# One fused transformer kernel on one core: the row scale of the mixer's norm applied after the products, the state stage's sums and exponentials made earlier

## The reference

```python
hn = rmsnorm(h, norm_mix_w[i])
proj = hn @ w_in[i]
q, k, v, z, xbc, dt_raw = jnp.split(proj, SPLITS, axis=-1)
att = chunk_band_attention(q, k, v, rel_bias[i])
ssd = ssd_mixer(z, xbc, dt_raw, conv_w[i], conv_b[i], dt_bias[i], a_log[i], d_skip[i], ssd_norm_w[i])
h = h + jnp.concatenate([att, ssd], axis=-1) @ w_out[i]
hn = rmsnorm(h, norm_mlp_w[i])
h = h + jnp.square(jax.nn.relu(hn @ w_ff1[i])) @ w_ff2[i]
```

## Time and profile before

| | us |
|---|---|
| median of 3 runs | 781.71 |
| the runs | 780.65, 781.71, 781.85 |
| the profiled execution | 780.67 |
| its span | 778.9 |
| TensorE busy in the span | 762.0 |
| DVE busy | 513.8 |
| ACT busy | 416.0 |
| POOL busy | 98.3 |

### The profile page before, as it was taken

One profiled execution on the slowest core, in us unless ns is written; L12 is line 12 of the kernel. 1 busy time (PEld: TensorE's weight loads), 2 busy tenths in 40 slices (PEclk: granted clock), 3 DMA queues, 4 the chain that ended last, 5 costly groups with the idle time before them and its releaser, 6 DMA issues.

```text
span 778.9 us, 12960 instructions
## 1 busy us (share of the span) xinstructions
PE 762.0 (98%) x5014; PEld 670.3 (86%) x5014; DVE 513.8 (66%) x816; ACT 416.0 (53%) x623; POOL 98.3 (13%) x74
## 2 busy tenths in 40 slices
PE   8999999999999999999999899999999999999997
PEld 7998877799978887999787699889777999999996
DVE  6985556666664558477866875787856755555554
ACT  5544445453664553446675567576655544444443
POOL 3341000000100004111300207700000000000002
PEclk9999999999999999999999999999999999999999
DMA  9965643344664544676833554765317575656541
GB/s 334 332 203 177 215 163 108 122 157 121 210 224 160 172 157 160 195 227 197 247 114 104 166 176 151 219 205 173 109 55 219 192 237 191 207 177 211 169 156 55
DMA packets 77659, 139.54 MB, mean 179 GB/s; under 512 B 7184, under 2 KB 15648, under 8 KB 77600
## 3 DMA queue, kind: packets, MB, share of 16 engines
q1 hardware_dynamic: 75744, 132.15, 52.4%
q0 software_dynamic: 1856, 6.57, 2.6%
HBM read 134.90 MB, written 1.06 MB: 175 GB/s over the span
## 4 chain that ended last, share of the span: by engine, by line
PE 87%; DVE 6%; issue 3%; POOL 2%; ACT 1%; DMA 1%; SPq 0%; POOLq 0%; ACTq 0%; DVEq 0%
PE acc L1081 13%; PE acc L1083 13%; PE acc L1082 13%; PE acc L1089 12%; PE acc L1091 12%; PE acc L1090 12%; DVE w_lo L810 2%; PE acc L1369 1%; PE acc L1403 1%; DMA raw<-in_w_in_even 1%; PE acc L1342 1%; PE acc L1282 1%; PE acc L1238 1%; PE acc L1353 1%; POOL b_lo L810 1%
## 5 line engine op out<-in xcount | busy, mean ns | idle before, releaser
L810 DVE TENSOR_TENSOR w_lo<-raw,w_hi 128x1024 fp32r<-128x1024 f32 (+1 forms) x224 | 275.3, 1245 | 171.3 <-ACT w_hi L790 90.2
L1089 PE MATMUL acc<-x_hi,w_hi 128*128 128x256 f32 x840 | 234.8, 280 | 1.5 <-DVE w_lo L810 1.1
L1091 PE MATMUL acc<-x_hi,w_lo 128*128 128x256 f32 x840 | 232.1, 276 | 0.0
L1090 PE MATMUL acc<-x_lo,w_hi 128*128 128x256 f32 x840 | 232.1, 276 | 0.0
L790 ACT ACTIVATE w_hi<-raw 128x1024 fp32r<-128x1024 f32 (+1 forms) x128 | 133.6, 1045 | 126.4 <-PE acc L1091 63.9
L780 ACT ACTIVATE w_hi<-raw 128x1024 fp32r<-128x1024 f32 x109 | 116.1, 1065 | 107.6 <-PE acc L1091 55.5
L1089 PEld LDWEIGHTS acc<-x_hi,w_hi 128*128 128x128 f32 x840 | 157.7, 188 | 4.1 <-issue 2.8
L1090 PEld LDWEIGHTS acc<-x_lo,w_hi 128*128 128x128 f32 x840 | 157.8, 188 | 0.8 <-issue 0.5
L1091 PEld LDWEIGHTS acc<-x_hi,w_lo 128*128 128x128 f32 x840 | 157.7, 188 | 0.0
L1081 PE MATMUL acc<-w_hi,cat_hi 128*128 128x512 f32 x272 | 108.9, 400 | 0.2 <-DVE w_lo L810 0.2
L1083 PE MATMUL acc<-w_hi,cat_lo 128*128 128x512 f32 x272 | 106.2, 390 | 0.0
(11 more groups left out here) (297 smaller groups left out, 903.0 us busy)
## 6 DMA issues: line engine op xcount, KB each, us to landing
raw<-in_w_ff SPq DMA_DIRECT2D x32, 1024.0 KB, 5.3
raw<-in_w_in_even SPq DMA_DIRECT2D x28, 1024.0 KB, 5.0
raw<-in_w_in_odd SPq DMA_DIRECT2D x16, 1024.0 KB, 5.4
raw<-in_w_in SPq DMA_DIRECT2D x16, 1024.0 KB, 5.6
raw<-in_w_out_even SPq DMA_DIRECT2D x12, 1024.0 KB, 5.4
raw<-in_w_out SPq DMA_DIRECT2D x4, 1024.0 KB, 5.3
raw<-in_w_in_even SPq DMA_DIRECT2D x4, 512.0 KB, 6.2
raw<-in_w_ukv_even SPq DMA_DIRECT2D x8, 256.0 KB, 3.2
```

The costliest lines, as they stand in the source:

```text
L810: ins = eng.tensor_tensor(lo, r, hi.bitcast(F32), ALU.subtract)
L1089: pe.matmul(o, wh[k][:, fs], hi[:, ka, :], start=start and f % 2 == 0, stop=False, skip_group_check=True)
L1090: pe.matmul(o, wh[k][:, fs], lo[:, ka, :], start=False, stop=False, skip_group_check=True)
L1091: ins = pe.matmul(o, wl[k][:, fs], hi[:, ka, :], start=False, stop=stop, skip_group_check=True)
```

## The change

The order of the plan and the place of two kinds of work change.

1. r is no longer applied to the rows ahead of the transposes. TensorE turns `res` itself; the products of v, dt, xBC, z, q and k are made from unscaled rows, and r enters where a chunk is read out of PSUM: as a per-row scale for v, z, dt and y·silu(z); as `r_row` (r spread over all partitions by one product with a diagonal, `mix_spread`) for q, k and xBC. Those read-outs of xBC, q and k go from ACT to DVE.
2. `v_rows` takes v's products with the high parts apart from those with the low parts; dt is made once, with 256 columns. The five filling products at the start go, the one ahead of the second transposes become four.
3. `ssd_cums` moves to c1, the four spreads (`ssd_spread`) behind it, into four buffers that lie over `cat2`. The decays of group 0 (`ssd_seg` 0) are made behind the last `conv_end`, those of group 1 behind z0b and ahead of z0's `epi`, 2 and 3 one and two pieces on. C·B, x and every near group lie a piece sooner; the far part lies inside z1b.
4. The norm of y is in two steps (`ssd_gate`, `ssd_scale`), its transposes lie in kb instead of V; some of the splits of weights wait until these steps are issued.

The diff, cut:

```diff
 RAW_SLOTS = 3
 WARM = 9
-BUSY_MIX = (5, 1)
+BUSY_MIX = 4
 LAG = 3
...
     step("mix_turn", 1)
-    step("rows_of", (rows_pieces["dt"], 0, 0, 8))
     step("rows_of", (rows_pieces["v"], 1, 0, 8))
     step("epi", rows_pieces["v"].chunk)
     step("rows_of", (rows_pieces["dt"], 1, 0, 8))
...
         if n:
             step("conv", 2 * (n - 1))
+            if n == 1:
+                step("ssd_cums", 0)
         else:
+            step("mix_spread", 0)
             step("dt_sum", c_dt)
             step("epi", c_dt)
             step("softplus", 0)
             step("conv", 2 * (n - 1) + 1)
         if n == 1:
             step("conv_end", 0)
+            step("ssd_spread", 0)
         if n == 2:
             step("conv", 4)
             step("conv_end", 1)
     parts[0]()
     step("conv", 5)
     step("conv_end", 2)
+    step("ssd_seg", 0)
     parts[1]()
     z_end = steps.pop()
-    step("ssd_cums", 0)
+    step("ssd_xs", 0)
+    step("ssd_seg", 1)
     steps.append(z_end)
-    between = [[("ssd_cb", 0), ("ssd_xs", 0), ("ssd_xs", 1)], [("ssd_rows", 0)], [("ssd_rows", 1)], [("ssd_rows", 2)], [("ssd_rows", 3)],
-               [("ssd_last", 0), ("ssd_gate", 0)], [("ssd_turn", 0)]]
+    between = [[("ssd_cb", 0), ("ssd_rows", 0), ("ssd_xs", 1), ("ssd_far", 0)], [("ssd_rows", 1), ("ssd_seg", 2), ("ssd_far", 1)],
+               [("ssd_rows", 2), ("ssd_seg", 3)], [("ssd_rows", 3)], [("ssd_last", 0), ("ssd_gate", 0)], [("ssd_turn", 0)], []]
     for f, sts in zip(parts[2:] + [second_v], between):
         one, two = by_halves(f)
         one()
         for st in sts:
             step(*st)
         two()
+        if ("ssd_gate", 0) in sts:
+            step("ssd_scale", 0)
     ys3 = []
     def second_out(k0, n, nk=4):
...
+            def v_rows(p, t):
...
+                wh, wl = weights_of(p)
+                def high(u, b):
+                    pe.wait_ge(*due("mix_hi", 4 * u + b + 1))
+                    for k in (2 * b, 2 * b + 1):
+                        xh, o = hi[:, k, u * P:(u + 1) * P], acc[:, p.chunk.pair, u, 0:p.cols]
+                        pe.matmul(o, xh, wh[k], start=k == 0, stop=False)
...
+                        high(0, b)
+                    return
+                for b in range(4):
+                    low(0, b)
+                    high(1, b)
+                for b in range(4):
+                    ins = low(1, b)
+                own(ins, "piece_used")
             def mix_turn(t):
                 if t:
-                    pe.wait_ge(*due("mix_lo", 4))
-                    keep_busy(acc[:, v_piece.chunk.pair, 1, :], BUSY_MIX[1])
-                rows = tmp[:, t * D:(t + 1) * D]
+                    keep_busy(acc[:, v_piece.chunk.pair, 1, :], BUSY_MIX)
                 for h in range(2):
-                    pe.wait_ge(*due("mix_scaled", 2 * t + h + 1))
...
                     for k in range(4 * h, 4 * h + 4):
-                        ins = pe.transpose(aux[:, k // 2, (k % 2) * P:(k % 2 + 1) * P], rows[:, k * P:(k + 1) * P], ident)
-                        if k % 2:
-                            own(ins, "mix_turned")
-                pe.wait_ge(*due("acc_read_dve", by_turn[v_piece.chunk.turn - 2].read_count))
+                        ins = pe.transpose(aux[:, 2 * t + h, (k % 4) * P:(k % 4 + 1) * P], res[:, t, k * P:(k + 1) * P], ident)
+                    own(ins, "mix_turned")
                 if t:
                     state["x"] += 1
...
                 elif kind == "mix_turn":
                     mix_turn(i)
+                elif kind == "mix_spread":
+                    pe.wait_ge(*due("mix_diag", 1))
+                    own(pe.matmul(aux[:, 3, 0:S], ones, gated[:, 1, :], start=True, stop=True), "mix_spread")
...
-                        pe.wait_ge(*due("far_ready", 1))
-                        for g in range(2):
-                            ins = pe.matmul(aux[:, 2 + g, :], cb[:, 2, g, :],
-                                            x_far[:, 8 * g:8 * g + 8, :].rearrange("p h n -> p (h n)"), start=True, stop=True)
-                        own(ins, "y_far_ready")
+                elif kind == "ssd_far" and i:
+                    pe.wait_ge(*due("far_ready", 1))
+                    for g in range(2):
+                        ins = pe.matmul(aux[:, g, :], cb[:, 2, g, :],
+                                        x_far[:, 8 * g:8 * g + 8, :].rearrange("p h n -> p (h n)"), start=True, stop=True)
+                    own(ins, "y_far_ready")
                 elif kind == "ssd_last":
...
                 elif kind == "mix_rows":
-                    row_squares(0)
-                    hi_prep(act, own, dt_piece.n)
-                    row_scaled(0)
+                    row_squares(0, 0)
                 elif kind == "mix_turn":
+                    if i:
+                        row_squares(1, 0)
+                        row_squares(1, 1)
                     row_hi(i)
                     if i == 0:
+                        row_squares(0, 1)
+                        hi_prep(act, own, dt_piece.n)
                         hi_first(act, own, conv_piece.n)
-                        row_squares(1)
-                        row_scaled(1)
                     else:
...
+                        act.wait_ge(*due("mix_r", T))
+                        for t in range(T):
+                            ins = act.activation(epi_dst(c)[:, t], a2[:, t], ACT.Copy, scale=mix_r[:, t:t + 1])
+                        own(ins, "acc_read_act")
+                    elif c.scaled and c.epilogue == "silu_tok":
+                        act.wait_ge(*due("piece_used", c.pieces[-1].n + 1))
+                        act.wait_ge(*due("mix_half", 1))
+                        for t in range(T):
...
                         own(act.activation(R3[:, 0:1024].rearrange("p (b n) -> p b n", b=2), a2, ACT.Square), "squares_ready")
                         own(act.activation(R3[:, 2048:3072].rearrange("p (b n) -> p b n", b=2), a2, ACT.Copy), "acc_read_act")
                     elif c.epilogue == "conv_in":
-                        act.wait_ge(*due("piece_used", c.pieces[-1].n + 1))
                         act.wait_ge(*due("pad_ready", 1))
-                        for b in range(2):
-                            f = c.info["dst"] + 2 * b
-                            ins = act.activation(conv_in[:, f:f + 2, 3:], a2[:, b, :].rearrange("p (f s) -> p f s", f=2), ACT.Copy)
-                        own(ins, "acc_read_act")
-                        own.wait()
+                        act.wait_ge(*due("acc_read_dve", c.read_count))
                         m = c.info["dst"] // 4
                         if m < 2:
...
                     act.wait_ge(*due("edge_ready", 1))
                     act.activation(ssd_c[:, 7, :], ssd_c[:, 7, :], ACT.Exp)
                     own(act.activation(ssd_c[:, 8, :], ssd_c[:, 8, :], ACT.Exp), "edge_exp")
-                elif kind == "ssd_rows":
+                elif kind == "ssd_seg":
                     b, g = i // 2, i % 2
                     cum = ssd_c[:, 6, 16 * b + 8 * g:16 * b + 8 * g + 8]
-                    if i >= 2:
-                        act.wait_ge(*due("y_near", i - 1))
-                    act.wait_ge(cum_spread[i % 2], 16 * (i // 2 + 1))
+                    act.wait_ge(cum_spread[i], 16)
                     for h in range(8):
...
                         continue
+                    elif c.epilogue == "conv_in":
+                        dve.wait_ge(*due("piece_used", c.pieces[-1].n + 1))
+                        dve.wait_ge(*due("row_scale", 1))
+                        for b in range(2):
+                            f = c.info["dst"] + 2 * b
+                            ins = dve.tensor_tensor(conv_in[:, f:f + 2, 3:], a2[:, b, :].rearrange("p (f s) -> p f s", f=2), rows_scale(2), ALU.mult)
+                            if b == 0:
+                                own(ins)
+                        own(ins, "acc_read_dve")
+                    elif c.scaled and c.epilogue == "copy_feat":
+                        dve.wait_ge(*due("piece_used", c.pieces[-1].n + 1))
+                        scale = DH ** -0.5 if c.info["dst"] == ("R3", 0) else 1.0
+                        dst = R3[:, c.info["dst"][1]:c.info["dst"][1] + 1024]
+                        own(dve.scalar_tensor_tensor(dst.rearrange("p (f s) -> p f s", f=4), a2.rearrange("p b (f s) -> p (b f) s", f=2), scale, rows_scale(4),
+                                                     ALU.mult, ALU.mult), "acc_read_dve")
                     elif c.epilogue in ("residual", "add"):
                         dve.wait_ge(*due("piece_used", c.pieces[-1].n + 1))
...
                     row_part(0, 1)
                     dve.wait_ge(*due("piece_used", last_out[1].n + 1))
                     row_add(1, 1)
                     row_part(1, 1)
                     row_moments(1)
                     row_centred(1)
-                    row_lo(0, 0, 2)
                     row_normed(1)
-                    row_lo(0, 2, 4)
```

(62 more changed lines are left out.)

151 lines of the change are left out of this document (88 added, 63 removed).

## The result

The changed kernel took **783.72 us** (median of 7 runs, 782.56 to 784.53) beside 781.71 for the kernel before (7 runs, 780.58 to 783.19): a ratio of 1.0027, 95% interval 1.0015 to 1.0039. It is slower by about 2 us, where 782.5 was forecast. Its profiled execution took 784.11, with a span of 782.2.

What follows compares the result with a forecast made beforehand. TensorE, busy 98% of the span, was taken as the bound, so only its waits or omitted work could give time. Terms -2.9 +0.46 +6.2 -3.0 = +0.8 on 781.71 gave 782.5 us, 8-in-10 range 779.0 to 785.0.

Steps and rivals of the forecast that it cites:

- Norm, -2.9: Norm ahead of the mixer: first convolution piece starts at 447.9 instead of 450.77, a gain of 2.9 us.
- Spread, +0.46: Spread of r on TensorE: one added 256-column product, costing 0.46 us.
- The chain behind t0: From the last xBC piece's end: last tanh at 10.65 us, z0's gate after 21.7, near 0 at 26.2.
- New waits, +6.2: State stage: C·B waits 0.6 us, near 0 3.2, far products 2.0, near 2 0.4; together 6.2 us.
- Waits removed, -3.0: State stage's old waits, including that at the normed rows' transposes, go with their refill: 3.0 us.
- The clock: Rival: granted clock falls to half in near 0's 3.2 us wait; about +2 us, 784.5; chance 0.13.
- the three signs by which the prediction was to be called wrong: Near 0 does not wait, norm's waits stay at 2.5 us, or granted clock shows 0.5 after near wait.
- a 3 us stretch without work: Program's end: granted clock at 0.50 by 776.5, 3 us after the last product ended at 773.45.
- 1.8 us of wait that did no harm: Norm's waits in the kernel before, 1.8 us the longest, left the clock at 2.4 GHz.
- The norm gives only 1 us: Rival: in the norm, second tile's rows or ACT's copies bind as now; 784.4 us; chance 0.12.
- POOL is late at z0a: Rival: at z0a, POOL's issues take longer while DVE is busy; +1, 783.5 us; chance 0.08.
- The ACT queue is short enough: Faster rival: group 0's mask ready 23 us after t0, near 0 and far waits vanish; 777.3; chance 0.17.

Runs made afterwards that it cites:

- e12: Changed kernel without the norm's four filling products: 784.60 us, ratio 1.0043 to the kernel before.
- e3: Changed kernel with group 1's exponentials behind z0's tanh on ACT, still ahead of qa's first high half: 782.87 us, ratio 1.0021 to the kernel before.
- e4: Changed kernel with group 1's exponentials moved behind qa's first high half and the first mask: 779.65 us, ratio 0.9978 to the kernel before.
- e2: Changed kernel with six filling products ahead of near 0 and three ahead of the far products: 782.07 us, ratio 1.0008 to the kernel before.
- e6: e4 with the far products half a piece and a half later, behind qa's first half: 780.45 us, ratio 0.9988 to the kernel before.
- e1: Changed kernel with six filling products ahead of near 0 only: 784.23 us, ratio 1.0034 to the kernel before.
- e9: Changed kernel with the state stage back in its old order, new norm and DVE's copies kept: 778.32 us, ratio 0.9958 to the kernel before.
- e11: e4 with the multiplication that makes x_far on POOL instead of DVE: 780.85 us, ratio 0.9992 to the kernel before.
- e5: Changed kernel with three filling products ahead of the far products only: 784.29 us, ratio 1.0036 to the kernel before.

## Why the prediction was right where it was, and what it lacked

- **Norm, -2.9.** Measured 2.79 (c0a at 447.98 for 447.9). The filling products cost nothing in time, as said, but they do more than that: without them the clock falls (e12).
- **Spread, +0.46.** 0.43 (453.53 to 453.96 in the trace).
- **The chain behind t0.** t0 is 482.65 in the changed kernel, the start of z0a. The tanh of chunk 2 starts 10.5 us later (10.65 forecast), DVE's gate of z0 21.55 (21.7), near 0 26.0 (26.2), and TensorE was there at 23.0 (23.0). This is the mechanism that was forecast, step by step. ACT's queue is the cause, as e3 and e4 show.
- **New waits, +6.2.** Near 0 2.88 and the far products 1.55, with refill 3.03 and 1.70 (3.2 and 2.0 forecast; the idle time ahead of x_far, put at 0.46, was 0.10); C·B 0.53, with refill 0.69 (0.6). Near 2 did not wait (0.4 forecast), not even at full clock in e2; where its queue is pushed further, in e6, it waits 1.49. Together 5.4.
- **Waits removed, -3.0.** This was the weak term: the wait at the transposes of the normed rows stayed (0.56 us, 0.73 with refill), though the profile was to show none there; I had taken it for covered by kb's half, but DVE's scaling still waited 0.94 us for POOL's power (1.17 in the kernel before). So 2.3. The rest went as said.
- **The sum** of these is -2.79 + 0.43 + 5.4 - 2.3, that is +0.8, as forecast, but only because two misses cancel, 0.8 too much in the new waits and 0.7 too much in those removed. That part is luck. e2, the same kernel at full clock, lies 0.6 above the kernel before (interval -0.1 to 1.3).
- **The clock, not in the sum.** It stood as a rival at 0.13 and came true with the forecast. A granted clock of 0.5 after the near wait is also one of the three signs by which the prediction was to be called wrong, and it came: the waits were right, the clock was not, and the time lies within 779.0 to 785.0 all the same. It should not have been a rival to the forecast but a term of it: 1.65 us by the medians (2.2 by the profiled executions), and 783.72 less 782.5 is 1.2. What I weighed was the length of the near wait against a 3 us stretch without work and 1.8 us of wait that did no harm. The row between those of the earlier trace rows would have said more:

```profile
776.00:776.50 0.50, 0.00 (x0) 0.00 (x0) 0.12 (x1) 0.13 (x1) 0.00 (x0) 0.61 1.04 401
```

A mean of 0.61 puts that fall at about 776.1, 2.7 us after the last product, and the wait forecast was 3.2. I also left out the second wait right behind, which brought the clock down by itself in e1, and the sixteen products of 64 columns between them, whose part is not shown. The Trainium skill, "TensorE: Matmul & The Clock Gate", section "Why this matters for your kernels", asks for short gaps between bursts; the trace of the changed kernel agrees with its wait of 2.88 us, while the waits of 2.41 us in e12 and 1.60 in e1 are shorter than those it warns of, and the clock fell all the same.
- **The other rivals.** "The norm gives only 1 us" and "POOL is late at z0a" did not happen: 2.79 us, and no wait at z0a. "The ACT queue is short enough" did not happen here; e4 made it happen by moving one step. Priced at 777.3 with both waits gone, it gave 778.1 to 779.7 at full clock, where the far products still wait 1.60.

The loss of 5.4 us against e9 is made up so: the starts behind waits (C·B, near 0, the far products, the normed rows) are 6.15 us late in the changed kernel, and those of e9's four waits (0.69, 0.40, 0.56 and 0.31, each with refill) 2.6; 3.5 of difference and 1.65 for the clock are 5.2, and 0.2 is within the measurement. What stays open: no profile shows where the clock fell in the slower runs of e6, e11 and the kernel before, nor whether near 0's small products had a part in it.

## What to carry to other kernels

When work is moved ahead in an in-order queue, ask first what stands behind it there: group 1's exponentials were wanted a piece later than z0's tanh and qa's high half, and putting them two entries further back took 4 us off, part of it the clock. A stage moved earlier gains only up to the engine that carries it; here DVE was full behind it, and the old order with its two waits taken out was the best of those tried. Where a change gives TensorE a new wait, count the clock as a term of the sum, and read the granted clock before looking for other causes.

## What the runs showed of the hardware

- The clock fell after waits much shorter than the one I had feared: in e1 in a wait of 1.60 us, behind sixteen 64-column products. In e4 the same wait behind the same products brought it down in some runs and not in others of one kernel.
- The stretches at 1.2 GHz came in two lengths, read from the windows: 6.8 us in the changed kernel and in e1 (511.4 to 518.2), and 3.4 us in e3 (511.0 to 514.4) and e5 (509.7 to 513.1). The execution of e12 has one of each (442.8 to 446.2 and 511.1 to 517.9).
- DVE's mask took 2.92 us instead of 1.22 beside a multiplication on POOL, and ended 1.08 us after it; qa's low half in e4 ended 1.08 us after POOL's too. Moving work from a full DVE to an idle POOL gained nothing.
